# One diffusion step on one core: backward S5 powers moved to VectorE, the first expert tile's rows picked and the last tile's rows spread by TensorE

## What is computed

```python
# S5, one direction; u: (B,L,G,I), c_c: (G,O,P) complex
_, xs = lax.associative_scan(_linear_combine, (a_seq, bu), axis=1, reverse=reverse)
y = jnp.einsum('gop,blgp->blgo', c_c, xs).real
# mixture: top-2 experts inside the best group, weights wts
combine = jnp.sum(jax.nn.one_hot(top_i, N_EXPERTS) * wts[..., None], axis=-2)
hid = jax.nn.silu(einsum('bld,edf->blef', h, w_gate)) * einsum('bld,edf->blef', h, w_up)
moe = einsum('blef,efd->bld', hid * combine[..., None], w_down)
x = x + gate2 * moe            # gate2 differs between sample and prompt tokens
y = _rms(x, final_norm_g)
```

## Time and profile before

| what | value |
|---|---|
| time, median of 3 runs | 1368.99 us (1368.93 to 1369.64) |
| the profiled execution: its own time, its span | 1369.18 us, 1367.5 us |
| busy share of the span | PE 87%, DVE 38%, ACT 16%, POOL 18% |
| PE busy, 100 to 200 us / 900 to 1000 us / 1300 to 1368 us | 79.81 / 68.80 / 12.29 us |
| granted TensorE clock in these three | 0.90 / 0.81 / 0.62 |
| PE busy, 500 to 600 us (attention) | 99.31 us |

### The profile page before, as it was taken

One profiled execution on the slowest core, in us unless ns is written; L12 is line 12 of the kernel. 1 busy time (PEld: TensorE's weight loads), 2 busy tenths in 40 slices (PEclk: granted clock), 3 DMA queues, 4 the chain that ended last, 5 costly groups with the idle time before them and its releaser, 6 DMA issues.

```text
span 1367.5 us, 14788 instructions
## 1 busy us (share of the span) xinstructions
PE 1183.4 (87%) x5797; PEld 576.5 (42%) x5797; DVE 519.0 (38%) x1204; ACT 225.3 (16%) x545; POOL 249.5 (18%) x341
## 2 busy tenths in 40 slices
PE   2798699899998999999999999899359999989930
PEld 1445455355665544444444444345223333333310
DVE  3666454856725503333212323245605111111118
ACT  2111012112444322222110101101001010100112
POOL 2058200510059520000000223310310000000020
PEclk9799899999999999999999999999569999999975
DMA  9421312103130262101221674850398999999742
GB/s 300 170 85 37 35 58 82 61 8 55 62 110 12 71 230 93 62 14 49 62 70 62 225 247 157 283 185 31 132 355 281 376 374 384 394 371 378 277 148 115
DMA packets 96333, 222.29 MB, mean 163 GB/s; under 512 B 9401, under 2 KB 11321, under 8 KB 95745
## 3 DMA queue, kind: packets, MB, share of 16 engines
q1 hardware_dynamic: 80256, 173.45, 35.5%
q0 software_dynamic: 14128, 41.01, 9.8%
q10 hardware_dynamic: 1872, 6.82, 1.2%
HBM read 190.77 MB, written 28.38 MB: 160 GB/s over the span
## 4 chain that ended last, share of the span: by engine, by line
PE 73%; DVE 10%; DMA 7%; POOL 5%; issue 2%; ACT 1%; SPq 1%; POOLq 0%; DVEq 0%; ACTq 0%
PE banks L809 15%; PE banks L1029 14%; PE banks L942 10%; PE banks L635 10%; PE banks L964 5%; PE banks L1025 4%; DMA REG<-w_gate 3%; PE banks L883 2%; PE banks L611 1%; PE banks L905 1%; DMA REG<-REG 1%; PE banks L893 1%; PE banks L621 1%; PE banks L766 1%; DMA REG<-norm_g 1%
## 5 line engine op out<-in xcount | busy, mean ns | idle before, releaser
L809 PE MATMUL banks<-wring,HT 128*128 128x512 f32 x480 | 217.0, 600 | 0.0
L635 PE MATMUL banks<-wring,HT 128*128 128x512 f32 (+1 forms) x480 | 197.4, 572 | 0.5 <-ACT REG L1292 0.5
L1029 PE MATMUL banks<-REG 128*32 128x512 f32 x1008 | 176.7, 601 | 3.6 <-DMA REG<-w_gate 3.6
L942 PE MATMUL banks<-wring,REG 128*128 128x512 f32 x320 | 139.4, 595 | 1.5 <-DVEq L413 1.5
L635 PEld LDWEIGHTS banks<-wring,HT 128*128 128x128 f32 x480 | 92.7, 195 | 99.0 <-issue 95.9
L809 PEld LDWEIGHTS banks<-wring,HT 128*128 128x128 f32 x480 | 88.5, 192 | 95.8 <-issue 93.4
L942 PEld LDWEIGHTS banks<-wring,REG 128*128 128x128 f32 x320 | 60.2, 190 | 78.1 <-issue 76.1
L1029 PE MATMUL banks<-wring,REG 128*32 128x512 f32 x432 | 77.3, 593 | 1.5 <-DMA REG<-w_gate 1.5
L964 PE MATMUL banks<-wring,REG 128*128 128x512 f32 x160 | 72.4, 611 | 6.0 <-DMA wring<-w_out 6.0
L1029 PEld LDWEIGHTS banks<-REG 128*32 128x32 f32 x1008 | 47.0, 111 | 72.3 <-issue 72.3
L611 PE MATMUL banks<-ident,REG 128*128 128x128 f32 x250 | 39.3, 312 | 25.6 <-DVEq L1748 13.9
(11 more groups left out here) (379 smaller groups left out, 1504.1 us busy)
## 6 DMA issues: line engine op xcount, KB each, us to landing
wring<-w_in SPq DMA_DIRECT2D x12, 2048.0 KB, 7.7
REG<-w_down SPq DMA_DIRECT2D x10, 2048.0 KB, 17.2
REG<-w_gate SPq DMA_DIRECT2D x9, 2048.0 KB, 21.8
HT<-w_ada SPq DMA_DIRECT2D x8, 2048.0 KB, 8.6
REG<-w_up SPq DMA_DIRECT2D x8, 2048.0 KB, 16.4
wring<-w_up SPq DMA_DIRECT2D x7, 2048.0 KB, 17.5
scratch_x<-REG POOLq DMA_DIRECT2D x17, 512.0 KB, 10.4
wring<-w_gate SPq DMA_DIRECT2D x4, 2048.0 KB, 16.3
```

Of the source, the lines that this page charges most:

```text
L635: last = mm(out[:, 0:cols], HT[:, k, P * t:P * t + P], w[:, k, 0:cols], start=k == 0, stop=k == KD - 1)
L809: last = mm(chan.bank(), HT[:, k, P * (i % NT):P * (i % NT) + P], gate[1][:, k, :], start=k == 0, stop=k == KD - 1)
L942: last = mm(out, x[:, k, P * t:P * t + P], w[:, k, :], start=k == 0, stop=k == 3)
L1029: last = mm(out[js, :], columns(k)[:, js], ws[j == 3][:, k, cols], start=k == 0, stop=k == ks - 1)
```

## The change

1. **S5.** The backward output powers move from POOL to DVE (`backward_powers`, behind F0). POOL starts `first_rotations` right after it has asked for SRAW, and the parameters of half 1 are asked for behind the TOE transfers.
2. **First tile.** Tile 0's rows are no longer fetched. DVE makes one-hot matrices PICK from the ranks, and PE multiplies the normed rows with them (`pick`), which gives the turned rows in PSUM banks 6 and 7. `up` of tile 0 now stands ahead of `rows` of tile 1, and `slots_of_choices` behind `rows` of tile 0.
3. **Outputs.** DVE empties both halves of each down product and multiplies by a gain row (GAIN: gate 2 of sample or prompt, by a mask from the new `prompt_rows`); ACT only issues the store.
4. **Last tile.** It is not stored. DVE makes weighted one-hot matrices LAST (`last_tile_rows`), PE turns them behind `rows` of tile 6, and at the end PE multiplies them with the gated last tile and DVE adds that to X2 (`add_last`). The gathers start when 12 tiles are stored. The root is taken once for all five tiles, `general_passes` stands behind the combining on DVE and ACT, and the final gain is fetched earlier.

The core of the diff (`prompt_rows` makes the mask in ten small DVE instructions on 128 x 256 or less and one on 128 x 1024; `keep_last` copies the turned matrices out of PSUM):

```diff
-                 ("out", 4, 1), ("rank", 0), ("logits", 3), ("turn", 4), ("logits", 4), ("rank", 1))
+                 ("out", 4, 1), ("rank", 0), ("logits", 3), ("turn", 4), ("logits", 4), ("pick", 0), ("rank", 1), ("pick", 1))
...
-        MOE_STEPS += [("rows", one), ("up", waiting), ("rows", two), ("gate", one), ("turn", waiting), ("down", waiting), ("rows", three),
+        MOE_STEPS += [("up", waiting), ("rows", one)] if one == 1 else [("rows", one), ("up", waiting)]
+        MOE_STEPS += [("rows", two), ("gate", one), ("turn", waiting), ("down", waiting), ("rows", three),
...
-            pe.wait_ge(cpw_step, 6 * hf + 6)
...
+        def pick(part):
+            lo, hi = ROUTE_PARTS[part]
+            pe.wait_ge(picked, part + 1)
+            if part == 0:
+                for half in range(2):
+                    mm(banks[:, 6 + half, :], PICK[:, NT - 1, :], NROWS[:, 0, 0:512], start=True, stop=False)
+            for t in range(lo, hi):
+                for k in range(KD):
+                    last = mm(banks[:, 6 + k // 4, P * (k % 4):P * (k % 4) + P], NROWS[:, t, P * k:P * k + P], PICK[:, t, :],
+                              start=False, stop=t == NT - 1 and k % 4 == 3)
+            if part:
+                last.then_inc(row_t, 1)
...
+        def turn_last():
+            pe.wait_ge(last_known, 1)
+            pe.wait_ge(col_d, LAST_TURN + 1)
+            pe.wait_ge(col_a, LAST_TURN + 1)
+            for t in range(NT):
+                last = nc.tensor.transpose(banks[:, t // 3, P * (t % 3):P * (t % 3) + P], LAST[t], ident[:])
+            last.then_inc(last_turned, 1)
...
+        for t in range(NT):
+            if t == 2:
+                pe.wait_ge(out_d, NTILES)
+                pe.wait_ge(out_a, NTILES)
+            if t >= 3:
+                pe.wait_ge(t_combined, t - 2)
+            for half in range(2):
+                pe.wait_ge(last_gated, half + 1)
+                last = mm(banks[:, SPREAD_BANK[t] + half, :], TURNED[:, t, :], GATED[:, 512 * half:512 * half + 512], start=True, stop=True)
+            last.then_inc(last_full, 1)
...
+        sp.wait_ge(gu_full, unit_of["up", NTILES - 3] + 1)
+        sp.dma_start(FG, a["final_norm_g"].rearrange("(o e) -> o e", o=1).broadcast_to([P, D])).then_inc(fin_in, 16)
         general_passes(sp, sp_pass)
-        sp.wait_ge(dn1, NTILES)
-        sp.dma_start(FG, a["final_norm_g"].rearrange("(o e) -> o e", o=1).broadcast_to([P, D])).then_inc(fin_in, 16)
...
-            act.wait_ge(dn1, n + 1)
-            if n >= 2:
-                act.wait_ge(out_wr[n % 2], 16 * (n // 2))
-            A(OUT[:, n % 2, 512:1024], banks[:, 6, :], ACT.Copy).then_inc(out_a, 1)
+            if t == NTILES - 1:
+                return
+            act.wait_ge(out_d, n + 1)
             act.wait_ge(out_a, n + 1)
-            act.wait_ge(out_d, n + 1)
             act.dma_start(scratch_out[CAP * t:CAP * t + CAP, :], OUT[:, n % 2, :]).then_inc(out_wr[n % 2], 16)
...
-            done(ts(CTN, CT, -1.0, None, ALU.mult))
-            dve.sem_inc(powers_ready, 1)
...
+        def powers_out(d, temp):
+            pw, ct = output_powers(d)
+            re, im = CPW[:, d, 0], CPW[:, d, 1]
+            going(tt(temp, ct[1], pw[1], ALU.mult))
+            done(tt(re, ct[0], pw[0], ALU.mult))
+            done(tt(re, re, temp, ALU.subtract))
+            going(tt(temp, ct[0], pw[1], ALU.mult))
+            done(tt(im, ct[1], pw[0], ALU.mult))
+            done(stt(flat3(im), flat3(im), -1.0, flat3(temp), ALU.mult, ALU.subtract))
+        def backward_powers(hf):
+            if hf:
+                dve.wait_ge(state_out, 64)
+            powers_out(1, CTMP_B)
+            dve.sem_inc(cpw_back, 1)
...
+        steps = dict(params=params, modulate=modulate, su=none, F0=lambda hf: (turn_F(hf, 0), backward_powers(hf)), F1=lambda hf: turn_F(hf, 1),
...
+            dve.wait_ge(dve_step, steps_so_far())
+            dve.wait_ge(bc_in, 64)
+            for t in range(lo, hi):
+                going(ts(PICK[:, t, :], PLACES, RANK[:, t, 0:1], MB[:, t, 0:1], ALU.is_equal, ALU.mult))
+            if part == 0:
+                going(V_.memset(PICK[:, NT - 1, :], 0.0))
+            dve.wait_ge(dve_step, steps_so_far())
+            dve.sem_inc(picked, 1)
...
-            dve.wait_ge(dn0, n + 1)
-            if n >= 2:
-                dve.wait_ge(out_wr[n % 2], 16 * (n // 2))
-            cp(OUT[:, n % 2, 0:512], banks[:, 5, :]).then_inc(out_d, 1)
+            done(stt(GAIN, GAIN_P, PROMPT_ROW[:, t:t + 1], BCG2[:, 0, :], ALU.mult, ALU.add))
+            if t == NTILES - 1:
+                combine(0)
+            for half, (full, emptied) in enumerate(((dn0, out_d), (dn1, out_a))):
+                ns = slice(512 * half, 512 * half + 512)
+                if t == NTILES - 1 and half:
+                    combine(1)
+                dve.wait_ge(full, n + 1)
+                if t == NTILES - 1:
+                    tt(GATED[:, ns], banks[:, 5 + half, :], GAIN[:, ns], ALU.mult).then_inc(last_gated, 1)
+                    dve.wait_ge(last_gated, half + 1)
+                    dve.sem_inc(emptied, 1)
+                    continue
+                if half == 0 and n >= 2:
+                    dve.wait_ge(out_wr[n % 2], 16 * (n // 2))
+                done(tt(OUT[:, n % 2, ns], banks[:, 5 + half, :], GAIN[:, ns], ALU.mult))
+                dve.sem_inc(emptied, 1)
...
+            for t in (0, 1, 2, 4, 3):
+                other = TURNED[:, 3, :] if t == 3 else LAST[3]
+                going(ts(LAST[t], PLACES, LAST_AT[:, t, 0:1], WP[:, 0, t:t + 1], ALU.is_equal, ALU.mult))
+                done(ts(other, PLACES, LAST_AT[:, t, 1:2], WP[:, 1, t:t + 1], ALU.is_equal, ALU.mult))
+                done(tt(LAST[t], LAST[t], other, ALU.add))
+            dve.sem_inc(last_known, 1)
...
+        def combine(t):
+            dve.wait_ge(t_y_in[t], 32)
+            for k in range(2):
+                y = YR_P[:, k, :] if t == NT - 1 else YR[:, t, k, :]
+                done(stt(X2[:, t, :], y, WP[:, k, t:t + 1], X2[:, t, :], ALU.mult, ALU.add))
+        def add_last(t):
+            dve.wait_ge(last_full, t + 1)
+            b = SPREAD_BANK[t]
+            done(tt(X2[:, t, :], X2[:, t, :], banks[:, b:b + 2, :].rearrange("p b c -> p (b c)"), ALU.add))
+            dve.sem_inc(t_combined, 1)
...
+            if (kind, t) == ("rows", 0):
+                slots_of_choices()
             if (kind, t) == ("up", 0):
-                slots_of_choices()
+                prompt_rows()
+            if (kind, t) == ("up", 2):
+                last_tile_rows()
+            if (kind, t) == ("rows", LAST_TURN):
+                keep_last()
+        combine(2)
+        combine(3)
+        add_last(0)
+        combine(4)
+        for t in range(1, NT):
+            add_last(t)
...
-        general_passes(dve, dve_pass)
-        def combine(t):
-            s, y = 0 if t < NS else 1, [YR[:, t, j, :] for j in range(2)]
-            dve.wait_ge(t_scaled, t + 1)
-            done(stt(y[0], y[1], WP[:, 1, t:t + 1], y[0], ALU.mult, ALU.add))
-            done(tt(y[0], y[0], BCG2[:, s, :], ALU.mult))
-            done(tt(X2[:, t, :], X2[:, t, :], y[0], ALU.add))
-            dve.sem_inc(t_combined, 1)
-        def final_rows(t):
-            dve.wait_ge(t_sq, t + 1)
-            y = root(t, small[:, t:t + 1])
-            stt(X2[:, t, :], X2[:, t, :], y, FG, ALU.mult, ALU.mult).then_inc(fin_ready, 1)
+        general_passes(dve, dve_pass, lambda: dve.wait_ge(sq_again, NT))
+        dve.wait_ge(t_sq, NT)
+        mean, y, u = (small[:, b:b + NT] for b in (8, 16, 24))
+        done(ts(mean, small[:, 0:NT], 1.0 / D, EPS, ALU.mult, ALU.add))
+        rsqrt(y, mean, u)
+        dve.wait_ge(fin_in, 16)
         for t in range(NT):
-            combine(t)
-            if t == 1:
-                dve.wait_ge(fin_in, 16)
-            if t >= 1:
-                final_rows(t - 1)
-        final_rows(NT - 1)
+            stt(X2[:, t, :], X2[:, t, :], y[:, t:t + 1], FG, ALU.mult, ALU.mult).then_inc(fin_ready, 1)
...
             if hf == 0:
                 for t in range(NT):
-                    if t == NT - 1:
-                        backward_output_powers(0)
                     pool.wait_ge(scr, t + 1)
...
             if hf == 0:
-                parameters_in(1)
                 first_rotations()
-            else:
-                backward_output_powers(1)
             pool.wait_ge(kp_ready, hf + 1)
             for s in range(Q):
                 pool.dma_start(TOE[16 * s:16 * s + 16, :, :],
                                KP[:, :, 7 - s:15 - s, :].rearrange("i g t o -> i g (t o)")).then_inc(toe_in, 16)
+            if hf == 0:
+                pool.wait_ge(cpw_back, 1)
+                parameters_in(1)
             pool.wait_ge(toe_in, 16 * Q * (hf + 1))
...
-        general_passes(pool, pool_pass)
+        pool.wait_ge(routing, GATHER_KNOWN)
+        pool.wait_ge(dn1, NTILES - 1)
         for b in range(2):
```

(30 more changed lines are left out.)

134 lines of the change are left out of this document (79 added, 55 removed).

## The result

The changed kernel takes 1320.5 us (median of four runs, 1319.5 to 1324.4) against 1369.0; the ratio is 0.9653 with a 95% interval of 0.9631 to 0.9674. The prediction was 1316 with a range of 1307 to 1330. The profiled span is 1319.4, 48.1 less than before. It helps to cut both spans at landmarks that both programs have, since the cuts show where the 48.1 came from. All numbers are differences of start times in the timelines.

A forecast was written before the change was run, and what follows sets the result against it. PE's work was taken as the bound nearly everywhere, so only shorter PE gaps or a shorter tail count: 12.4 + 7.3 + 10 + 23.8 = 53.5 off 1369.18 gives 1315.7, forecast 1316 us, range 1307 to 1330.

The forecast's parts named there:

- A, half 0: S5 stage, half 0: backward powers on DVE and earlier rotations on POOL bring TOE at 128.5; 12.4 us gained.
- the fifth store's landing: S5 half 0, POOL: landing of the fifth channel tile's store, taken as 2.04 us ahead of SRAW and the rotations.
- rival 1: S5 half 0: POOL's rotations don't overlap with DVE, TOE at 137, 3.9 gained there, time 1324.5; chance 0.12.
- the sum's 121.5: S5 half 0: time of TOE if the rotations last 24.2 as before, without waiting for DVE's products.
- Half 1: S5 stage, half 1: F0's operations quicker, PE's wait of 6.42 gone, turns gain about 1; 7.3 us gained.
- B: First expert tiles: first product at about 993.2 rather than 1009.25, gate 1 9.9 sooner; 10 us gained.
- rival 2: Expert loop: the weight stream, not PE, sets the pace; B's 10 lost and 3.7 more, time 1329.7; chance 0.12.
- The cost of turning LAST at nothing: Expert loop, PE: LAST's five transposes cost nothing, at most 0.3 us, since PE waits there for w_gate.
- The loop's DVE work at nothing: Expert loop: DVE's output work grows from 0.69 to about 3.0 a tile beside a down product; costed at nothing.
- C: Tail behind PE's last down product: 53.7 us falls to 29.9; 23.8 us gained.
- value load and branch of `general_passes` beyond the square 1.0: Tail, DVE: loading the value and branching adds 1.0 us behind ACT's square of the last tile, ahead of the root.
- The bound of 2.1: Tail, DVE: upper bound for load and branch beyond the square, from the shortest DMA landing of 2.04.

The follow-up runs named there:

- s5_alone: The kernel before with the S5 part of the change alone (backward powers on DVE, rotations ahead of the parameters); 1348.5 us, ratio 0.9853.
- rows2_late: The changed kernel with tile 2's rows turned behind gate 1 instead of ahead of it; 1319.9 us, ratio 0.964.
- after_again: The changed kernel unaltered, run once more beside the others; 1320.3 us, ratio 0.9646.
- half_weights: The changed kernel with each weight block behind the first seven fetched by half, so results are not the reference's; 1316.7 us, ratio 0.9605.
- gain_four: The changed kernel with four GAIN operations in place of one ahead of twelve outputs; 1320.5 us, ratio 0.9663.
- branch_early: The changed kernel with DVE's TOP_COUNT load and branch past the general passes moved ahead of its last slot_out; 1323.6 us, ratio 0.9669.
- branch_at_gate: The changed kernel with DVE's TOP_COUNT load and branch past the general passes moved ahead of its last gate step; 1319.1 us, ratio 0.964.

## Why the prediction was right or wrong

**A, half 0: right in kind, 2 too much.** The six products took 1.36 each and fitted; DVE's F1 began at 95.37, the very time of before. TOE came at 129.68, forecast 128.5. The step that failed is the fifth store's landing, taken as 2.04 from the earlier trace rows: that row is only what was left of it when POOL came to wait. POOL waited 6.83 now, and with 0.7 more for the copies ahead of them, made beside DVE, the rotations began at 102.80, 5.5 later than the 97.3 of the sum. From their first product they took 26.9 against 24.2, by the contention that rival 1 is about. The 7 us between the sum's 121.5 and the 128.5 taken were room for contention alone; it used 2.7 of them. That TOE came within 1.2 all the same is luck: one term was too large where the other was too small. The Trainium skill (SBUF — State Buffer, "SBUF: two separate sides") says that the loser waits for the whole of the other's instruction, and the products of 1.34 beside DVE's 1.36 agree, with 0.28 apiece when DVE is idle. Rival 1 priced it wrongly as a full stop: POOL had a turn between any two of DVE's, and F1 was over at 102.65, ahead of the first rotation. Little is left to gain there: DVE's gathering of the kernels, for which TOE waits too, ended at 127.20, only 2.5 ahead of TOE. Behind TOE, PE took 16.0 in place of 15.1, of which 0.9 is the transfers' own landing (14.24 to DVE's first copy, 13.37 before).

**Half 1: right.** 7.3 gained, 7.3 forecast, F's operations at 1.22 with nothing of POOL beside them. s5_alone shows that the gains of both halves reach the end, within the 2 us to which the loop repeats.

**B: right in sum, its middle partly wrong.** The first expert product came 16.6 sooner against the landmark, and gate 1 9.7 (forecast 16.0 and 9.9, before's frame without A). But what held gate 1 was not DVE's `slots_of_choices` and `prompt_rows`, as the prediction's working put it. DVE's copy of tile 1 came 0.8 behind the turn (996.17, turned by 995.3), which the next landing hid; PE waited for the landings of tile 1 and tile 2 (3.54 and 2.09), and the weights of gate 1 land just behind (rows2_late). Three things were due within 3 us, so either account gives the number. Of rival 2 a part may have come true: what is 9.7 at gate 1 is 9.2 at the last turn (8.2 and 7.2 in after_again). Gate 1 itself ran 8.65 in place of 7.07, at a low clock, and PE waited 2.9 to 5.3 in all for w_gate, with the half clock behind; but the kernel before has 5.1 of such waits too, and no run parts what made the difference. The prediction let the later asks move with PE; what it left out is that the stream has no room, with a DMA share of 1.04, so a block that is asked for sooner need not land sooner. That reading is argued, not shown. half_weights prices the stream at 5.4 to 7.5, most of which the kernel before pays too. The cost of turning LAST at nothing stands: the five transposes take 0.73 ahead of a wait that would be there without them.

**The loop's DVE work at nothing: right.** gain_four adds three times as much GAIN for no time.

**C: the mechanism right, 2.5 too much.** The step that failed is "value load and branch of `general_passes` beyond the square 1.0". Load and branch took 5.16 of DVE in branch_early; in the changed kernel DVE's gap is 4.21, 2.9 of it behind the square. The bound of 2.1, taken from the shortest landing in the earlier trace rows, was too low: a transfer's landing is no bound on a branch. The Trainium skill (Runtime: NRT & Kernel Launch, "Instruction fetch mechanics") says that a taken branch beyond the pages at hand waits for a fetch. The trace agrees with that in kind, 4.21 and 5.16 of DVE with no releaser, though no run here parts the load from the branch, or shows the fetch itself. The other 0.6 is small waits of DVE for PE (0.34) and hand-overs.

The sum: 53.5 forecast, 48.1 in the profile; 2.1 of the miss is A, 0.8 B, 2.5 C. By the second profile, after_again, A's half 0 gains 10.6 and B 7.2, so B's share isn't known better than to 2 us. The 1316 for a measured 1320.5 thus has its misses all on one side: A and B lie within their bounds, C, at 21.3, just under its 21.5.

## What to carry to other kernels

A gap of TensorE that another engine's work opened is worth its whole length even 1,000 us before the end, as long as what follows is TensorE's own work. Ahead of the expert loop, whose weight stream ran at a DMA share of 1.04, 0.5 of a gain of 9.7 was lost again behind it, and 1.0 of 8.2 in a second profile. A DMA wait in a trace is only what was left of the transfer when the engine arrived: if the engine will come sooner, the landing has to be taken from the issue. Code that is skipped isn't free: put its branch where that engine waits anyway.

## What the runs showed of the hardware

- Loading a value and branching past the general passes, with the branch taken, cost DVE 5.16 us (branch_early); in the changed kernel the gap that holds the same two was 4.21.
- Two products of 128 x 64 on POOL took 2.68 beside DVE's operations of 1.36 and 0.56 without them.
- Behind waits for weights of 2.87 (changed kernel) to 4.58 us (s5_alone) TensorE worked for some us at half its clock (granted 0.50), and a product group of 7.0 took 1.7 to 2.8 longer; behind one of 1.64 (branch_at_gate) it took 7.0.
- The same code reached its first store of S5 channels after 64.3 to 69.3 us in the runs profiled, which is one reason why ratios of this kernel can't tell 3 us.
